# Attention scores that carry minus the softmax scale, and sums of probabilities taken for two heads at once, in a one-core Trainium2 kernel

## What is computed

```python
def block_attention(q, k, v):
    ...
    scale = HEAD_DIM ** -0.5

    def one_block(qblk):
        s = jnp.einsum('bkgqd,bskd->bkgqs', qblk, k).astype(jnp.float32) * scale
        p = jax.nn.softmax(s, axis=-1).astype(v.dtype)
        return jnp.einsum('bkgqs,bskd->bkgqd', p, v)
```

## Time and profile before

| | us |
|---|---|
| median of 3 runs (lowest 3138.42, highest 3140.06) | 3138.7 |
| the profiled execution, its own time | 3139.49 |
| span of the profiled execution, first to last instruction | 3137.8 |
| first to last exponential of attention (start times in the span) | 623.7 to 1545.7 |
| TensorE matmuls busy | 2974.2 (95% of the span) |
| TensorE weight loads busy | 2739.5 (87%) |
| VectorE busy | 1852.7 (59%) |
| ScalarE busy | 1674.1 (53%) |
| GpSimd busy | 700.5 (22%) |

### The profile page before, as it was taken

The page is one execution under the profiler, slowest core; times in us unless marked ns, Lnnn a source line. Parts: engine busy times, 40 slices in busy tenths (PEclk is TensorE's granted clock), DMA queues, the critical chain, the costliest instruction groups (busy, mean ns, idle before and its releaser), DMA issues. The chain is left out here.

```text
span 3137.8 us, 57856 instructions
## 1 busy us (share of the span) xinstructions
PE 2974.2 (95%) x20880; PEld 2739.5 (87%) x20880; DVE 1852.7 (59%) x3261; ACT 1674.1 (53%) x3227; POOL 700.5 (22%) x878
## 2 busy tenths in 40 slices
PE   8999997899999999999899969999999999999996
PEld 5888886688888888888788759999999999999996
DVE  5222225788888888888643387655555555555555
ACT  4222223677777777777534336544444454454454
POOL 1333335632323223232000011111111111111104
PEclk9999999999999999999899959999999999999998
DMA  7211116501010010010164336666666666666657
GB/s 256 84 68 68 68 60 203 178 14 35 17 30 20 17 33 17 20 30 17 45 208 148 120 96 201 188 194 189 194 197 189 196 196 189 191 199 195 194 184 285
DMA packets 320130, 394.76 MB, mean 126 GB/s; under 512 B 30260, under 2 KB 276488, under 8 KB 319016
## 3 DMA queue, kind: packets, MB, share of 16 engines
q1 hardware_dynamic: 307416, 356.18, 34.5%
q0 software_dynamic: 12240, 36.77, 4.8%
q10 hardware_dynamic: 384, 0.62, 0.1%
HBM read 319.60 MB, written 74.06 MB: 125 GB/s over the span
## 5 line engine op out<-in xcount | busy, mean ns | idle before, releaser
L2877 DVE TENSOR_TENSOR e_w_lo<-e_raw,e_w_hi 128x2048 fp32r<-128x2048 f32 x189 | 433.1, 2291 | 411.7 <-ACT e_w_hi L2794 411.7
L92 PE MATMUL e_ps<-e_x_hi,e_w_hi 128*128 128x272 f32 x2048 | 601.6, 294 | 2.6 <-issue 2.6
L94 PE MATMUL e_ps<-e_x_hi,e_w_lo 128*128 128x272 f32 x2048 | 593.4, 290 | 0.0
L93 PE MATMUL e_ps<-e_x_lo,e_w_hi 128*128 128x272 f32 x2048 | 590.0, 288 | 0.0
L1709 DVE TENSOR_TENSOR a_pT_lo<-a_ps_t,a_pT_hi 128x512 fp32r<-128x512 f32 (+1 forms) x648 | 367.8, 600 | 137.2 <-ACT a_pT_hi L1618 136.9
L1618 ACT ACTIVATE a_pT_hi<-a_ps_t 128x512 fp32r<-128x512 f32 (+1 forms) x648 | 319.3, 532 | 160.2 <-PE a_ps_t L1486 155.1
L92 PEld LDWEIGHTS e_ps<-e_x_hi,e_w_hi 128*128 128x128 f32 x2048 | 386.3, 189 | 3.0 <-issue 3.0
L93 PEld LDWEIGHTS e_ps<-e_x_lo,e_w_hi 128*128 128x128 f32 x2048 | 387.0, 189 | 0.0
L94 PEld LDWEIGHTS e_ps<-e_x_hi,e_w_lo 128*128 128x128 f32 x2048 | 385.8, 188 | 0.0
L2794 ACT ACTIVATE e_w_hi<-e_raw 128x2048 fp32r<-128x2048 f32 x189 | 360.6, 1908 | 0.0
L1486 PE MATMUL a_ps_t<-ident,a_prob 128*128 128x128 f32 x2184 | 329.6, 280 | 29.9 <-DVE a_pT_lo L1709 19.1
(11 more groups left out here) (358 smaller groups left out, 5492.3 us busy)
## 6 DMA issues: line engine op xcount, KB each, us to landing
e_raw<-in_w_gate SPq DMA_DIRECT2D x64, 1024.0 KB, 5.0
e_raw<-in_w_up SPq DMA_DIRECT2D x64, 1024.0 KB, 5.0
e_raw<-in_w_down SPq DMA_DIRECT2D x64, 1024.0 KB, 5.0
s_ret<-p_pr SPq DMA_DIRECT2D x17, 768.0 KB, 3.6
p_raw<-in_w_in SPq DMA_DIRECT2D x8, 1152.0 KB, 18.7
o_cT<-s_ct SPq DMA_DIRECT2D x17, 512.0 KB, 4.9
s_x<-o_x SPq DMA_DIRECT2D x17, 512.0 KB, 5.0
s_xn<-o_xn SPq DMA_DIRECT2D x17, 512.0 KB, 3.6
```

What stands on the lines that cost most here:

```text
L92: nc.tensor.matmul(out, w_hi, x_hi, start=first, stop=False)
L93: nc.tensor.matmul(out, w_hi, x_lo, start=False, stop=False)
L94: return nc.tensor.matmul(out, w_lo, x_hi, start=False, stop=last)
L2877: nc.vector.tensor_tensor(w_lo[n % RING][:, :, :], raw[n % RING][:, :, :], w_hi[n % RING][:, :, :].bitcast(F32), ALU.subtract).then_inc(w_ ...
```

## The change

The queries are multiplied by minus the softmax scale when they are split, so the scores in PSUM are already scaled and negated. Then the smallest score of a row is the offset that the exponential needs, and the exponential multiplies the score by -1. The three-column reduction writes `a_nm` itself, and the multiplication behind it is gone, with its semaphore `max_all`. The sums of the segments are kept for four heads in place of two, and `total` runs in odd steps alone, for the pair of heads.

```diff
+SCALE = HD ** -0.5
+assert HD == 64
...
     def queries_hi(self, act):
         act.wait_ge(self.q_in, 16)
-        self.nc.scalar.activation(self.q_parts[:, :, 0, :], self.q_row[:, :, :], ACT.Copy).then_inc(self.q_hi_ok, 1)
+        self.nc.scalar.activation(self.q_parts[:, :, 0, :], self.q_row[:, :, :], ACT.Copy, scale=-SCALE).then_inc(self.q_hi_ok, 1)
...
     def queries_lo(self, dve):
         dve.wait_ge(self.q_hi_ok, 1)
-        self.nc.vector.tensor_tensor(self.q_parts[:, :, 1, :], self.q_row[:, :, :], self.q_parts[:, :, 0, :].bitcast(F32),
-                                     ALU.subtract).then_inc(self.q_lo_ok, 1)
+        self.nc.vector.scalar_tensor_tensor(out=self.q_parts[:, :, 1, :], in0=self.q_row[:, :, :], scalar=-SCALE,
+                                            in1=self.q_parts[:, :, 0, :].bitcast(F32), op0=ALU.mult, op1=ALU.subtract)\
+            .then_inc(self.q_lo_ok, 1)
...
-        mx, nm = k.sb("a_mx", [P, 2, 4]), k.sb("a_nm", [P, 2])
-        sums, total_s, rsum = k.sb("a_sums", [P, 2, 3]), k.sb("a_total", [P, 2]), k.sb("a_rsum", [P, NQ])
+        mx, nm = k.sb("a_mx", [P, 2, 3]), k.sb("a_nm", [P, 2])
+        sums, total_s, rsum = k.sb("a_sums", [P, 2 * GROUP, 3]), k.sb("a_total", [P, 2, GROUP]), k.sb("a_rsum", [P, NQ])
...
-        max_ok, max_all, nmax_ok = k.sem("a_max_ok"), k.sem("a_max_all"), k.sem("a_nmax_ok")
+        max_ok, nmax_ok = k.sem("a_max_ok"), k.sem("a_nmax_ok")
...
-                          "turn": lambda n: n in turns_of(i), "total": lambda n: True,
+                          "turn": lambda n: n in turns_of(i), "total": lambda n: h % GROUP == GROUP - 1,
...
                 if seg == segs_of(i)[0]:
                     act.wait_ge(nmax_ok, n + 1)
-                    if not (isinstance(n, int) and n < 2):
-                        act.wait_ge(sum_ok, n - 1)
+                    if not (isinstance(n, int) and n < 2 * GROUP):
+                        act.wait_ge(sum_ok, i * NGRP + h // GROUP - 1)
                 nc.scalar.activation(seg_probs(i, h, seg), seg_scores(seg, seg_width(i, seg)), ACT.Exp,
-                                     bias=nm[:, h % 2:h % 2 + 1], scale=scale,
-                                     accum_out=sums[:, h % 2, seg:seg + 1]).then_inc(exped[seg], 1)
+                                     bias=nm[:, h % 2:h % 2 + 1], scale=-1.0,
+                                     accum_out=sums[:, h % (2 * GROUP), seg:seg + 1]).then_inc(exped[seg], 1)
...
                 dve.wait_ge(scored[seg], n + 1)
-                nc.vector.tensor_reduce(mx[:, h % 2, seg:seg + 1], seg_scores(seg, seg_width(i, seg)), AXY, ALU.max)\
+                nc.vector.tensor_reduce(mx[:, h % 2, seg:seg + 1], seg_scores(seg, seg_width(i, seg)), AXY, ALU.min)\
                     .then_inc(max_ok, 1)
                 if seg == segs_of(i)[-1]:
                     dve.wait_ge(max_ok, (n + 1) * 3 if not (isinstance(i, int) and i == NT) else NT * NQ * 3 + h + 1)
-                    nc.vector.reduce_max(mx[:, h % 2, 3:4], mx[:, h % 2, min(segs_of(i)):3], AX).then_inc(max_all, 1)
-                    dve.wait_ge(max_all, n + 1)
                     if not (isinstance(n, int) and n < 2):
                         dve.wait_ge(exped[SEG_ORDER[-1]], min(n - 1, NT * NQ) if isinstance(n, int) else n - 1)
                         if isinstance(n, int) and n - 1 > NT * NQ:
                             dve.wait_ge(exped[2], n - 1)
-                    nc.vector.tensor_scalar(nm[:, h % 2:h % 2 + 1], mx[:, h % 2, 3:4], -scale, None, ALU.mult)\
+                    nc.vector.tensor_reduce(nm[:, h % 2:h % 2 + 1], mx[:, h % 2, min(segs_of(i)):3], AX, ALU.min)\
                         .then_inc(nmax_ok, 1)
...
                 dve.wait_ge(exped[segs_of(i)[-1]], n + 1)
-                nc.vector.reduce_sum(total_s[:, h % 2:h % 2 + 1], sums[:, h % 2, min(segs_of(i)):3], AX).then_inc(sum_ok, 1)
-                dve.wait_ge(sum_ok, n + 1)
-                nc.vector.reciprocal(rsum[:, h:h + 1], total_s[:, h % 2:h % 2 + 1]).then_inc(rsum_ok, 1)
+                grp = h // GROUP
+                of = slice(grp % 2 * GROUP, (grp % 2 + 1) * GROUP)
+                nc.vector.reduce_sum(total_s[:, grp % 2, :], sums[:, of, min(segs_of(i)):3], AX).then_inc(sum_ok, 1)
+                dve.wait_ge(sum_ok, i * NGRP + grp + 1)
+                nc.vector.reciprocal(rsum[:, grp * GROUP:(grp + 1) * GROUP], total_s[:, grp % 2, :]).then_inc(rsum_ok, 1)
```

More of the change, by code:

```diff
@@ L1180, in attention @@
         NK = NTA + 1
-        scale = HD ** -0.5
         keys = k.sb("a_keys", [P, 2, NKV, NK * P], F32R)
@@ L1597, in queries_hi @@
                     act.wait_ge(scored[2], (i - 1) * NQ + 1)
-                nc.scalar.activation(q_parts[:, :, 0, :], q_row[:, :, :], ACT.Copy).then_inc(q_hi_ok, 1)
+                nc.scalar.activation(q_parts[:, :, 0, :], q_row[:, :, :], ACT.Copy, scale=-SCALE).then_inc(q_hi_ok, 1)
             def exps(i, h, seg):
@@ L1674, in queries_lo @@
                 dve.wait_ge(q_hi_ok, i + 1)
-                nc.vector.tensor_tensor(q_parts[:, :, 1, :], q_row[:, :, :], q_parts[:, :, 0, :].bitcast(F32),
-                                        ALU.subtract).then_inc(q_lo_ok, 1)
+                nc.vector.scalar_tensor_tensor(out=q_parts[:, :, 1, :], in0=q_row[:, :, :], scalar=-SCALE,
+                                               in1=q_parts[:, :, 0, :].bitcast(F32), op0=ALU.mult, op1=ALU.subtract)\
+                    .then_inc(q_lo_ok, 1)
             def maxima(i, h, seg):
```

## The result

| | before | with the change |
|---|---|---|
| median of 5 and 5 runs, us | 3140.06 | 3125.49 |
| lowest to highest, us | 3138.42 to 3145.21 | 3123.55 to 3128.01 |
| the profiled execution, us (span) | 3139.49 (3137.8) | 3125.61 (3123.9) |
| ratio, 95% interval | | 0.9950 (0.9938 to 0.9962) |

What follows compares the result with a forecast made beforehand. TensorE leads with small holes, and the change pays only where one ends on VectorE. Looped and unrolled tiles 13.8, last tile 1.1, first head 0.2: 15.1 us off the 3138.7 us median gives 3123.6, range 3117.5 to 3131.5.

Steps and rivals of the forecast that it cites:

- the short distance: Rival: the removed multiplication on VectorE was worth only 0.12 us start to start; 8.5 us gained, 3130.2 us; chance 0.08.
- Steps 1 and 3 do not: In these two heads of a tile ScalarE's chain holds the exponential, so only 0.03 us each is gained.
- six steps pay: Rival: the exponential is not the limit in steps 1 and 3, which add 4.8 us; 3118.8 us; chance 0.12.
- Step 7, 0.24 us: In this head the exponential idles for a_nm and follows by 0.24 us in 13 looped tiles, 0.19 in three unrolled.
- Step 5, 0.19 us: In this head TensorE's hole of 0.75 us at turn 2 shrinks by 0.19 us.
- Steps 0 and 2, 0.19 each: In these heads TensorE's holes at turn 2, 0.56 and 0.38 us, shrink by 0.19 us each.
- two steps less: Rival: steps 0 and 5 pass nothing on, held by ScalarE's own chain; 6.1 us less gained, 3129.7 us; chance 0.12.
- Totals at nothing: The 68 sums and 68 reciprocals removed lie between lo 1 and lo 2, under a wait for ScalarE; counted as 0.
- the slower rival: Rival: the minimum over PSUM costs more than the maximum; 3144 us at 10% more, 3161 at 20%; chance 0.04.
- nothing measurable: Rival: every TensorE hole is refilled by the next dependency; only 1.3 us at the ends remain, 3137.4 us; chance 0.10.
- Unrolled tiles and the context tile: Three unrolled attention tiles gain 0.82 us each; the last, context tile, a pure chain, gains 1.1 us over about 6 heads.
- All behind moves up whole: The stages behind attention start earlier by attention's whole gain, with 1 us either way for clock and loads.

Runs made afterwards that it cites:

- dependent_twice: The full change with two chained multiplications by 1 put between the small reduction and a_nm; ratio to before 1.0076, tile 57.69 us.
- late_exp: The full change plus a one-column ScalarE copy that nothing reads ahead of a head's first exponential; ratio to before 0.9979, tile 56.01 us.
- offset_only: The full change, but with totals for every head as in the kernel before; ratio to before 0.9942, tile 55.37 us.
- one_ahead: The full change plus one fill of one column that nothing reads, once at the start of attention; ratio to before 0.9947, tile 55.47 us.
- totals_only: The kernel before with only the totals for two heads at once; ratio to before 1.0000, tile 56.56 us.
- no_sum_wait: The full change without the exponential's second wait, the one on the totals; ratio to before 0.9938, tile 55.46 us.

## Why the prediction was right, and which of its steps were not

**The price of the operation** was right. It said 0.19 us, since the second operation reads what the first wrote, against 0.12 by the short distance. dependent_twice shows 0.19 for a link of the chain and 0.18 to 0.20 in six steps. The rival of the short distance falls, and so does a semaphore between chained operations that costs nothing extra: on this chain the operation that waits for the one before starts 0.19 us behind it, the one that does not, 0.11 to 0.13.

**"Steps 1 and 3 do not"** was wrong: they gave 0.17 and 0.12 us. The reading behind it, that their exponential "starts when hi 1 is done, not when a_nm is", took a start 0.06 us behind the end of the row before for an engine that went straight on. Rows of one engine that don't wait overlap: in the changed kernel the exponential starts 0.12 us before hi 1's listed end. The rest of that step was right: late_exp shows that in 1 and 3 the exponential is what TensorE feels, and not lo 0. So the rival "six steps pay" describes the mechanism (1.17 us a tile by its terms), and with the offset alone (1.08) it nearly came out. The Trainium skill's page "Perfetto Trace Analysis", section "DVE / Act Engine Instruction (TENSOR_ADD, Activation, etc)", says that the reported end of such an instruction is when its write is acknowledged, and that the next may begin reading before that. By this a start behind the listed end does not prove a busy engine, and the trace agrees: 0.06 us behind that end before, 0.12 us ahead of it after.

**Step 7, 0.24 us**, was 0.18. The forecast said that the register instruction that stood between reduction and multiplication "now stands ahead of the reduction, beside a maximum of 1.08 us", at no cost. It does not stand beside the maximum: it carries the wait for it, starts when it is done, and the small reduction starts 1.21 us behind the big one instead of 1.11. The 0.10 us only moved from behind the small reduction to ahead of it, and a_nm came 0.19 us sooner, what a link is worth. Step 1 of the changed kernel has the same 0.10 us more, and didn't have it before; it came with the totals, since in offset_only the distance in step 1 is still 1.13. The path was right in step 7; the term was mis-sized by that instruction.

**Step 5, 0.19 us**, was 0.07: the queries' low half starts 0.22 us behind the reduction where it started 0.10 behind a_nm. No price of an operation was wrong, and "the ends are 0 and 0.05" for the fused form held at 0. The distance is not a property of the operations: one_ahead, with the same ones in the same order, takes 0.12 us away and 0.11 of it reaches the step, and offset_only gained 0.20 in this step. The cause stays open.

**Steps 0 and 2, 0.19 each**, were 0.17 and 0.18; lo 0 carries step 2 in the main, and step 0 as far as is known. The rival "two steps less" (0 and 5) falls: step 0 paid here, and step 5 paid 0.20 with the offset alone. **Totals at nothing** was 0.1 us of a tile too good: not the operations, which lie under the cover of lo 2's wait, but the register instruction ahead of the exponential, which with the new threshold carries the wait for a_nm in steps 0, 3 and 5 too; in totals_only only step 3, the one of them that follows the exponential, becomes clearly longer. **The minimum** costs what the maximum did (1.08 us), so the slower rival falls, and "nothing measurable" with it.

**Unrolled tiles and the context tile.** The forecast gave 0.82 us to an unrolled tile. Counted from turn 0 to turn 0, tiles 0, 1 and 15 gave 1.39, 1.01 and 1.42. Tile 1 is the clean one: there the thresholds are constants, no register instruction carries a wait, and each of the six steps gave 0.15 to 0.19. Tile 0 is not: in one_ahead it gave 0.41, as its step 0 took 7.15 us where it takes 6.21 in the change, and why steps 1 and 7 of tile 15 gave 0.35 us each, not 0.17 or so, is not known. The context tile gave 0.9 us up to the last output, for 1.1.

Summed, attention gained 11.5 in the loop, 3.8 and 0.9, 16.2 us by the timelines, against the 15.1 of the forecast. **"All behind moves up whole"**, with 1 us either way, was the last miss: 2.0 us came back, some 0.9 of it in the projection's start at half clock and the rest not located. So the close sum, 14.6 us for 15.1, is in good part luck: in a looped tile steps 1 and 3, counted 0.23 us too low, and steps 0, 2, 5 and 7, counted 0.21 too high, cancel, and behind attention, where nothing was counted, 2.0 us came back against the 1.1 that attention had gained beyond the forecast. The price of the link and the chain that it was taken from were no luck.

## What to carry to other kernels

Price an instruction that is taken off a serial chain by its start-to-start distance and count every step where either branch behind it reaches the busiest engine; a start just behind the former row's end is not proof of a busy engine, only a start before that end is. In a loop, look up in the trace which instruction carries each wait on the chain: where it is a register instruction and not the operation itself, the operation starts some 0.08 to 0.10 us later, and a change of a threshold elsewhere can move the wait there. And an operation that still stands in the chain is worth more moved under another's wait than its neighbour shortened: the queries' low half gave 0.45 us a tile in one step, half of what the change gave in six.

## What the runs showed of the hardware that had not been expected

- Behind a row of ScalarE that it doesn't wait for, the exponential starts 0.12 us before that row's listed end (1022.98 against 1023.10).
- Where a register instruction carries the wait for a result and the operation behind it does not, the operation starts 0.08 to 0.10 us later: 0.27 instead of 0.19 us from a_nm to the exponential, and 1.21 instead of 1.11 from big to small reduction. Where the operation carries the wait itself, the small reduction shows no such cost in any looped step; the exponential still shows 0.21 to 0.26 us in some steps of no_sum_wait and offset_only, which is open.
- From a_nm to the queries' low half, the same instructions in the same order took 0.22 us in one program (the change) and 0.10 in another (one_ahead) that has a single small instruction, a one-column tile and a semaphore more, in every pass of the loop.
